# A hybrid attention and MLP block on one core: the first tile by row blocks, the mixing output's products spread in front of the weighing, and the MLP's start laid over the last attention tile

## The chip, the core and the metric

The program runs on one core of one Trainium2 chip. The metric is device time in microseconds (us) of one execution. The engines of the core are named as the profile names them: PE is TensorE's matmuls (PEld its weight loads), DVE VectorE, ACT ScalarE, POOL GpSimd, SP SyncE, which here only starts DMA transfers.

## The reference

One decoder layer for 2048 tokens of width 1024, in float32, cut to what matters here:

```
hn = rmsnorm(h, g_mix_pre)
z = hn @ w_in                                # 1024 x 1604
q, k, v, qi, ki, w, zp = split(z)            # rope on q, k, qi, ki
score = sum_h w[h] * relu(qi[h] @ ki.T)      # causal, 4 index heads
sel = top_k(score, 256)                      # keys kept for each query
attn = softmax(q @ k[sel].T) @ v[sel]        # 8 heads of 64, 2 kv heads
pool = pool_mixer(zp)
mix = concat(attn, pool) @ w_o               # 1024 x 1024
h = h + rmsnorm(mix, g_mix_post)
m = square(relu(rmsnorm(h, g_mlp_pre) @ w_up)) @ w_down      # hidden 4096
h = h + rmsnorm(m, g_mlp_post)
h = h + rmsnorm(sigmoid(h @ w_ple_gate) * (p @ w_ple_proj), g_ple_post)
```

Nearly every large product is written as three products of a high and a low float32 part (high by high, high by low, low by high).

## The kernel before, in words

The work stands in the program for each engine in its order, by hand, with semaphores between engines. A planner fills in the search for the kept keys (a threshold found in 32 rounds, each a count over the scores on DVE and on ACT) at numbered spots of the two stages below.

**Projection stage**, 16 tiles of 128 tokens. At the start SP starts five small loads, x for tiles 0 and 1, and the eight row blocks of w_in (128 rows each, w_in_raw). ACT makes each block's high part (w_in_hi, L986), DVE its low part (w_in_lo, L1442). DVE first computes the angles of the rotations (L1242 to L1256), for which ACT then takes the sine (L910). x is squared (L956), scaled (L1262) and transposed by PE (L1703) into hnT_hi (ACT, L941) and hnT_lo (DVE, L1267). Then PE computes four column groups of z one after the other, each over all eight row blocks (L1732).

**Attention stage**, 16 tiles of 8 heads, each head in 1 to 4 blocks of up to 512 keys; a step is one block of one head. In a step PE makes scores of a later step (L1754, L1755), transposes the probabilities of the step after next (L1840, turn_probs), and weighs the values with those of this step (L1854, weigh), for which it waits until ACT has copied them out of PSUM (probsT, L1071). DVE adds the mask to the scores as they come (L1484) and runs its half of the search round (L1346, then L1354 and L1363); ACT runs the exponential (L1058) and its half of the round (L968). After weigh come the index products of the search (L1754, L1755 with qi), and at the last block of heads 2 to 5 four products of the mixing output of the tile before (w_o, L1874, output_projection), 16 for a tile.

**MLP stage**, 4 chunks of 512 tokens. Weights come through a ring of two w_raw buffers of 1 MB, and are split into pieces (w_hi by ACT, L1114, w_lo by DVE, L1554) that PE takes one by one (L1732); the input hn_lo, hn_hi is loaded from DRAM and split (L1119, L1574). Before its first piece the program does the whole tail of tile 15: transpose of the attention output, its 16 output products, norms, the transposes of tiles 14 and 15 (L1891), their stores, and then the loads of the MLP (L740, L704).

Of the kernel before, what the change touches and what calls it, by code (L numbers as in the profile page):

```python
# [7 lines left out]
P = 128  # L8
F32 = mybir.dt.float32
# [8 lines left out]
Q_HEADS = 8  # L18
# [29 lines left out]
def hybrid_block(nc, x, p, positions, g_mix_pre, w_in, w_pool, pool_scale, w_o, g_mix_post,  # L48
# [32 lines left out]
    with ExitStack() as ctx:  # L81
# [80 lines left out]
        sbB("score_tail_kept", [P, S])  # L162
        block_max = sbB("block_max", [P, 2, 4])
# [12 lines left out]
        kept = sbB("kept", [P, S])  # L176
        drop = sbB("drop", [P, 2, S], BF16)
        weighed = sbB("weighed", [P, 3, 512])
# [14 lines left out]

        w_raw = sbC("w_raw", [P, 2, 2048])
        w_hi = sbC("w_hi", [P, 4, 1024], F32R)
        w_lo = sbC("w_lo", [P, 4, 1024], F32R)
        hn_hi = sbC("hn_hi", [P, K, CH], F32R)
        hn_lo = sbC("hn_lo", [P, K, CH], F32R)
        square = sbC("square", [P, 2, CH])
# [4 lines left out]
        hid_hi = sbC("hid_hi", [P, QF, CH], F32R)  # L204
        hid_lo = sbC("hid_lo", [P, QF, CH], F32R)
        g_mlp_row = sbC("g_mlp_row", [P, D])
        g_ple_row = sbC("g_ple_row", [P, D])
        p_in = sbC("p_in", [P, CT, PLE])
# [8 lines left out]
        w_in_ld = [sem("w_in_ld_low"), sem("w_in_ld_high")]  # L217
# [200 lines left out]

        AHEAD_BLOCKS = 2
# [74 lines left out]

        def mix_bank(i, n):
            return n if i == T - 1 else 0

        def norm_bank(i, n):
            return 2 + n if i >= T - 2 else 0
# [62 lines left out]
        def _(sp):  # L562
            def row_over_partitions(dst, src):
                return sp.dma_start(dst, src.to_broadcast([P, D]))

            sp.dma_start(pos_i[:], positions[0].rearrange("(t p) -> p t", p=P),
                         allow_slow_non_contiguous=True).then_inc(small_ld, 16)
            for dst, src in ((g_pre_col, g_mix_pre), (pool_scale_col, pool_scale), (g_mlp_col, g_mlp_pre)):
# [4 lines left out]
            def load_x(i, u):  # L573
                sp.dma_start(x_in[:, u, :], x_tiles[i]).then_inc(x_ld[u], 16)

# [3 lines left out]

            load_x(0, 0)  # L580
            load_x(1, 1)
            for k in range(K):
                sp.dma_start(w_in_raw[:, k, :], w_in[0, k * P:(k + 1) * P, :]).then_inc(w_in_ld[k // (K // 2)], 16)
# [65 lines left out]

            sp.wait_ge(zp_ps, T)  # L650
# [15 lines left out]
            for m, (H, b) in enumerate(steps):  # L666
# [16 lines left out]
                for t in mask_load_at.get(m, ()):  # L683
                    load_mask(t)
            load_pool(T - 1)
            store_h2(T - 2)
            load_x_row(T - 1)
            for i in range(T - 3, T):
                if i == T - 1:
                    store_h2(i)  # L690
                store_hn2T(i)

            sp.wait_ge(h2_st, 16 * T)
            hold()
            sp.wait_ge(hn2T_st, 16 * T)
            hold()
            loads = [0]

            def load_raw(width, src):
                n = loads[0]  # L700
                loads[0] += 1
                if n >= 2:
                    sp.wait_ge(w_lo_rdy, 2 * (n - 2) + 2)
                sp.dma_start(w_raw[:, n % 2, :].rearrange("p (k f) -> p k f", f=width), src).then_inc(raw_ld[n % 2], 16)  # L704

            def load_up(q, n):
                f = QF * q + 2 * n
                load_raw(2 * P, w_up[0, :, P * f:P * (f + 2)].rearrange("(k q) f -> q k f", q=P))

            def load_down(q, n):  # L710
                half, f = n // 2, QF * q + 4 * (n % 2)
                load_raw(512, w_down[0, P * f:P * (f + 4), 512 * half:512 * (half + 1)].rearrange("(a q) d -> q a d", q=P))

            def load_gate(n):
                half, k = n // 2, 4 * (n % 2)
                load_raw(512, w_ple_gate[0, P * k:P * (k + 4), 512 * half:512 * (half + 1)].rearrange("(a q) d -> q a d", q=P))

            def load_embed():
                n = loads[0]
                loads[0] += 1  # L720
                sp.wait_ge(w_lo_rdy, 2 * (n - 2) + 2)
                for k in range(KP):
                    sp.dma_start(w_raw[:, n % 2, :].rearrange("p (h k d) -> p h k d", h=2, k=KP)[:, :, k, :],
                                 w_ple_proj[0, P * k:P * (k + 1), :].rearrange("q (h d) -> q h d", h=2)).then_inc(embed_ld, 16)

            def load_tail():
                for n in range(GATE // 2):
                    load_gate(n)
                load_embed()

            for c in range(NCH):
                for q in range(QUARTERS):
                    if q == 2:
                        if c > 0:
                            sp.wait_ge(pT2_ps, 2 * c)
                            sp.wait_ge(out_st, 16 * CT * c)
                        sp.dma_start(p_in[:], p[0, 0, bass.ts(c, CH), :].rearrange("(a q) d -> q a d", q=P)).then_inc(p_ld, 16)
                        sp.dma_start(h2[:], h2_dram[bass.ts(c, CH), :].rearrange("(a q) d -> q a d", q=P)).then_inc(h2_ld, 16)
                    if c == 0 and q == 0:
                        sp.dma_start(hn_lo[:].bitcast(F32), hnT_dram[:, :, bass.ts(0, CH)]).then_inc(hn2T_ld, 16)  # L740
# [1326 lines left out]
```

## Time and profile before

| | |
|---|---|
| median of 3 runs | 3249.56 us (3245.02 to 3249.63) |
| the profiled execution's own time | 3245.62 us |
| its span | 3243.8 us |
| PE, DVE, ACT, POOL busy | 2958.4, 1719.7, 1384.8, 390.2 us |
| mean granted PE clock | 0.945 |

The span runs from the first to the last instruction; the execution's own time has 1.8 us more. Busy shares are means over stages that have different limits.

### The profile page before, as it was taken

The numbers are of one execution on the slowest core, as the hardware profiler recorded it, in microseconds if no ns is written. First come the engines' busy times: TensorE is split into PE (matmuls) and PEld (weight loads), VectorE is DVE, ScalarE is ACT, GpSimd is POOL, SyncE is SP. The second block draws the span as 40 slices with busy tenths as digits, with TensorE's granted clock in tenths as the row PEclk, the third lists the DMA queues.
The fourth block names the chain that finished last, engine by engine and source line by source line (L and its number), as shares of the span: only waits on it lengthen the run. The fifth ranks groups of instructions, "written<-read, shape, count | busy, mean of one in ns | idle before, by whom it ended". The sixth has DMA issues, their size and how long they took to land.

```text
span 3243.8 us, 37680 instructions
## 1 busy us (share of the span) xinstructions
PE 2958.4 (91%) x14264; PEld 2407.2 (74%) x14264; DVE 1719.7 (53%) x3405; ACT 1384.8 (43%) x2202; POOL 390.2 (12%) x447
## 2 busy tenths in 40 slices
PE   5999977788788898899699999999999999999987
PEld 4887755566666676787588888888888888888875
DVE  3376778686777776832333344533445334453344
ACT  3252546575747547655322243322433224332232
POOL 1233331213040040000000001000010000100001
PEclk9999988889897887899899999999999999999998
DMA  3111142111110110111424233333323333233321
GB/s 122 61 49 54 38 126 69 36 59 44 40 50 28 41 41 11 45 33 43 149 91 134 94 117 104 117 126 102 117 97 124 124 104 117 92 130 123 103 92 39
DMA packets 224627, 266.50 MB, mean 82 GB/s; under 512 B 58176, under 2 KB 160320, under 8 KB 224448
## 3 DMA queue, kind: packets, MB, share of 16 engines
q1 hardware_dynamic: 222144, 255.72, 25.0%
q10 hardware_dynamic: 2304, 8.39, 0.6%
q8 instruction: 113, 1.85, 0.2%
q14 instruction: 66, 0.54, 0.1%
HBM read 224.07 MB, written 40.01 MB: 81 GB/s over the span
## 4 chain that ended last, share of the span: by engine, by line
PE 79%; DVE 7%; issue 7%; ACT 4%; POOL 2%; DMA 1%; SPq 0%; DVEq 0%; ACTq 0%; POOLq 0%
PE bank L1732 58%; PE bank L1874 6%; PE bank L1854 6%; PE bank L1754 3%; PE bank L1840 2%; PE bank L1755 2%; ACT kept L968 2%; DVE kept L1346 1%; PE bank L1703 1%; DVE probs L1484 1%; ACT probsT L1071 1%; POOL score L868 1%; DVE too_few L1354 1%; DMA w_in_raw<-in_w_in 1%; ACT score_tail L968 0%
## 5 line engine op out<-in xcount | busy, mean ns | idle before, releaser
L1554 DVE TENSOR_TENSOR w_lo<-w_raw,w_hi 128x1024 fp32r<-128x1024 f32 x296 | 361.5, 1222 | 582.2 <-ACT w_hi L1114 582.1
L1114 ACT CAST w_hi<-w_raw 128x1024 fp32r<-128x1024 f32 x296 | 308.5, 1043 | 661.4 <-PE bank L1732 641.5
L1854 PE MATMUL bank<-values,probsT 128*128 128x64 f32 x2176 | 335.3, 301 | 150.9 <-ACT probsT L1071 124.2
L1854 PEld LDWEIGHTS bank<-values,probsT 128*128 128x128 f32 x2176 | 314.6, 220 | 177.3 <-ACT probsT L1071 163.6
L1732 PE MATMUL bank<-hn_hi,w_hi 128*128 128x512 f32 x1024 | 400.2, 391 | 20.8 <-DVE hn_lo L1574 20.8
L1732 PE MATMUL bank<-hn_hi,w_lo 128*128 128x512 f32 x1024 | 398.9, 390 | 0.0
L1732 PE MATMUL bank<-hn_lo,w_hi 128*128 128x512 f32 x1024 | 398.9, 390 | 0.0
L1732 PE MATMUL bank<-w_hi,hid_hi 128*128 128x512 f32 x1024 | 398.7, 389 | 0.0
L1732 PE MATMUL bank<-w_hi,hid_lo 128*128 128x512 f32 x1024 | 398.4, 389 | 0.0
L1732 PE MATMUL bank<-w_lo,hid_hi 128*128 128x512 f32 x1024 | 398.4, 389 | 0.0
L1484 DVE CUSTOM_DVE_ANT_0 probs<-bank,mask 128x384 f32<-128x384 f32 (+3 forms) x320 | 193.7, 607 | 234.3 <-PE bank L1755 232.5
L968 ACT ACTIVATE kept<-score,threshold 128x1024 bf16<-128x1024 f32 (+4 forms) x160 | 251.9, 1574 | 112.2 <-DVE threshold L1363 91.8
L1346 DVE TENSOR_SCALAR_CACHE_REDUCE kept<-score,threshold 128x896 bf16<-128x896 f32 (+4 forms) x160 | 267.6, 1673 | 0.7
L1172 ACT ACTIVATE square<-bank 128x512 f32<-128x512 f32 x128 | 76.5, 598 | 405.5 <-PE bank L1732 405.4
L1874 PE MATMUL bank<-wo_sb,mixT_t 128*128 128x512 f32 x512 | 247.0, 628 | 2.2 <-ACT h_t L1036 1.1
L1630 DVE CAST hid_hi<-square 128x512 fp32r<-128x512 f32 x128 | 56.1, 438 | 360.3 <-ACT square L1174 360.3
L1732 PEld LDWEIGHTS bank<-hn_hi,w_hi 128*128 128x128 f32 x1024 | 192.6, 188 | 61.0 <-DVE w_lo L1554 21.2
L1732 PEld LDWEIGHTS bank<-hn_hi,w_lo 128*128 128x128 f32 x1024 | 192.5, 188 | 40.0
L1732 PEld LDWEIGHTS bank<-hn_lo,w_hi 128*128 128x128 f32 x1024 | 192.7, 188 | 39.5
L1732 PEld LDWEIGHTS bank<-w_hi,hid_hi 128*128 128x128 f32 x1024 | 192.2, 188 | 40.1
L1732 PEld LDWEIGHTS bank<-w_hi,hid_lo 128*128 128x128 f32 x1024 | 192.2, 188 | 39.8
L1732 PEld LDWEIGHTS bank<-w_lo,hid_hi 128*128 128x128 f32 x1024 | 192.2, 188 | 39.7
(200 smaller groups left out, 4983.1 us busy)
## 6 DMA issues: line engine op xcount, KB each, us to landing
w_raw<-in_w_up SPq DMA_DIRECT2D x64, 1024.0 KB, 5.7
w_raw<-in_w_down SPq DMA_DIRECT2D x64, 1024.0 KB, 5.0
w_raw<-in_w_ple_gate SPq DMA_DIRECT2D x16, 1024.0 KB, 5.1
x_in<-in_x SPq DMA_DIRECT2D x16, 512.0 KB, 3.6
q_t<-q_scratch SPq DMA_DIRECT2D x32, 256.0 KB, 3.7
x_t<-in_x SPq DMA_DIRECT2D x16, 512.0 KB, 4.3
h_scratch<-h_t SPq DMA_DIRECT2D x16, 512.0 KB, 2.9
hnT_scratch<-hn2T_t SPq DMA_DIRECT2D x16, 512.0 KB, 3.8
```

Of the source, the lines that this page charges most:

```text
L968: nc.scalar.activation(junk[:, 0:P * (t + 2)], score_of(t + 1), ACT.Sign, scale=-1.0, bias=threshold[:, 1:2].bitcast(F32), accum_out=below ...
L1114: nc.scalar.copy(piece_parts(p, w_hi[:, p % 4, :]), raw_piece(p)).then_inc(w_hi_rdy, 1)
L1172: nc.scalar.activation(square[:, f % 2, :], bank[:, UP[q % 2][f % 2], :], ACT.Relu).then_inc(relu2_step, 1)
L1346: nc.vector.tensor_scalar(junk[:, 0:P * (t + 1)], score_of(t), threshold[:, 0:1].bitcast(F32), -float(P), ALU.is_lt, ALU.add, accum_out=be ...
L1484: nc.vector.tensor_tensor_reduce(out=probs[:, H % 3, o:o + w], in0=bank[:, ring_bank[("s", H, b)], 0:w], in1=mask[:, i % 2, o:o + w], scal ...
L1554: nc.vector.tensor_tensor(piece_parts(p, w_lo[:, p % 4, :]), raw_piece(p), piece_parts(p, w_hi[:, p % 4, :]).bitcast(F32), ALU.subtract).t ...
L1732: ins = nc.tensor.matmul(dst, lhs[a], rhs[b], start=(first and n == 0), stop=(last and n == 2))
L1754: nc.tensor.matmul(dst, hi, k_parts[:, key, o:o + w], start=True, stop=False)
L1755: return nc.tensor.matmul(dst, lo, k_parts[:, key, o:o + w], start=False, stop=True)
L1840: last = nc.tensor.transpose(bank[:, 1 + m % 3, a * P:(a + 1) * P], probs[:, H % 3, o + a * P:o + (a + 1) * P], ident[:])
L1854: last = nc.tensor.matmul(bank[:, 4, h * HEAD:(h + 1) * HEAD], probsT[:, m % 3, a * P:(a + 1) * P], values[:, kt, HEAD * kv:HEAD * (kv + 1 ...
L1874: last = nc.tensor.matmul(bank[:, mix_bank(i, n), :], mixT_t[:, k, :], wo_sb[:, k, n * 512:(n + 1) * 512], start=(k == 0), stop=(k == K - 1))
```

## The change

Three places of the program change; no arithmetic is added or left out.

Start: x of tile 0, g_pre_col and four row blocks are loaded first, with a semaphore for each row block; the angles and the sine are computed behind tile 0's products; PE takes tile 0's products row block by row block for all four column groups. Middle: the output products of a tile are laid out one to three to a step over the steps of heads 2 to 5 (tiles with one block a head: eight in one step) and they and the index products stand ahead of weigh. Seam: chunk 0's input and the first two weight buffers are loaded at the start of tile 15, split in its last eight steps, and the tail of tile 15 is called piece by piece between the MLP's first pieces. The buffers are laid out anew so that what is loaded early lies over what is no longer used.

```
+            def project_first_tile():
+                for k in range(K):
+                    if k % 4 == 0:
+                        pe.wait_ge(hnT_lo_rdy, k // 4 + 1)
+                    pe.wait_ge(w_in_lo_rdy, k + 1)
+                    for b, lo, hi, done_sem in (...four column groups...):
+                        last = split_product(...)
+                    if k == 5:
+                        transpose_x(1)
@@ order of DVE at the start (ACT alike)
             norm(0, 0)
+            split_weights(range(0, 1))
+            evacuate_hnT(0, 0)
+            evacuate_hnT(0, 1)
+            split_weights(range(1, 4))
+            norm(1, 1)
+            split_weights(range(4, K))
+            evacuate_hnT(1, 0)
+            evacuate_hnT(1, 1)
+            rotations()
+            norm(2, 0)
@@ a step of PE in the attention stage
+                for i_mix, n, k in mix_at.get(m, ()):
+                    output_projection(i_mix, n, range(k, k + 1))
+                search_part(EARLY_SPOTS + m)
                 weigh(m)
-                search_part(EARLY_SPOTS + m)
-                    if h in (2, 3):
-                        output_projection(i - 1, 0, range(4 * (h - 2), 4 * (h - 1)))
-                    if h in (4, 5):
-                        output_projection(i - 1, 1, range(4 * (h - 4), 4 * (h - 3)))
@@ SP, at the first step of tile 15
+                    load_hn(0)
+                    load_up(0, 0)
+                    load_up(0, 1)
@@ ACT, a step of tile 15
+                if m > FIRST_PARTS:
+                    act.wait_ge(ring_ps, ring[LAST_SCORE] + 1)
+                split_input(0, first_input(m))
+                for n in first_weights(m):
+                    split(n)
+            def attention_tail(p):          # PE's; called behind piece p
+                if p == 0:
+                    transpose_o(T - 1)
+                if p in (1, 2):
+                    output_projection(T - 1, p - 1, range(K))
+                if p == 3:
+                    for n in range(2):
+                        transpose_hn2(T - 2, n)
+                if p == 9:
+                    for n in range(2):
+                        transpose_hn2(T - 1, n)
```

The order of DVE's instructions from the end of the angles on (COPY rot) before, in the first microseconds of the program:

```order
L1256 COPY rot<-turns 128x1
L1260 TENSOR_SCALAR ms<-ss 128x1
L1262 TENSOR_SCALAR x_in<-x_in,rstd 128x1024
L1442 SCALAR_TENSOR_TENSOR w_in_lo<-w_in_raw,g_pre_col,w_in_hi 128x1604 x8
L1260 TENSOR_SCALAR ms<-ss 128x1
L1262 TENSOR_SCALAR x_in<-x_in,rstd 128x1024
L1267 TENSOR_TENSOR hnT_lo<-bank,hnT_hi 128x512 x2
```

And DVE from its first instruction on in the changed kernel:

```order
L1298 TENSOR_SCALAR ms<-ss 128x1
L1300 TENSOR_SCALAR x_in<-x_in,rstd 128x1024
L1506 SCALAR_TENSOR_TENSOR w_in_lo<-w_in_raw,g_pre_col,w_in_hi 128x1604
L1305 TENSOR_TENSOR hnT_lo<-bank,hnT_hi 128x512 x2
L1506 SCALAR_TENSOR_TENSOR w_in_lo<-w_in_raw,g_pre_col,w_in_hi 128x1604 x3
L1298 TENSOR_SCALAR ms<-ss 128x1
L1300 TENSOR_SCALAR x_in<-x_in,rstd 128x1024
L1506 SCALAR_TENSOR_TENSOR w_in_lo<-w_in_raw,g_pre_col,w_in_hi 128x1604 x4
L1305 TENSOR_TENSOR hnT_lo<-bank,hnT_hi 128x512 x2
L1487 CAST pos_f<-pos_i 128x16
```

Tile 0's hnT_lo moved from behind eight low parts to behind one, and the angles from the front to behind tile 1's hnT_lo.

PE before, two steps of tile 5 (heads 2 and 3, two blocks of 384 keys a head), from scores to scores:

```order
L1754 MATMUL bank<-k_parts,q_hi 128x384
L1755 MATMUL bank<-k_parts,q_lo 128x384
L1840 MATMUL bank<-ident,probs 128x128 x3
L1854 MATMUL bank<-values,probsT 128x64 x3
L1874 MATMUL bank<-wo_sb,mixT_t 128x512 x4
L1754 MATMUL bank<-k_parts,q_hi 128x384
L1755 MATMUL bank<-k_parts,q_lo 128x384
L1840 MATMUL bank<-ident,probs 128x128 x3
L1818 MATMUL bank<-ident,q_t 128x128 x4
L1854 MATMUL bank<-values,probsT 128x64 x3
```

PE in the changed kernel, the same two steps:

```order
L1833 MATMUL bank<-k_parts,q_hi 128x384
L1834 MATMUL bank<-k_parts,q_lo 128x384
L1934 MATMUL bank<-ident,probs 128x128 x3
L1968 MATMUL bank<-wo_sb,mixT_t 128x512 x3
L1948 MATMUL bank<-values,probsT 128x64 x3
L1833 MATMUL bank<-k_parts,q_hi 128x384
L1834 MATMUL bank<-k_parts,q_lo 128x384
L1934 MATMUL bank<-ident,probs 128x128 x3
L1912 MATMUL bank<-ident,q_t 128x128 x4
L1968 MATMUL bank<-wo_sb,mixT_t 128x512 x3
L1948 MATMUL bank<-values,probsT 128x64 x3
```

Of the eight products of one half (n = 0), which stood as four behind the weighing of every second step, three, three and two now stand ahead of the weighing in three steps that follow each other.

ACT before, from the last copy of a mixing output in tile 15 to the tail:

```order
L1036 COPY h_t<-bank 128x512
L1071 COPY probsT<-bank 128x512 x4
L1052 COPY hn2T_t<-bank 128x512
L1071 COPY probsT<-bank 128x512 x3
L1052 COPY hn2T_t<-bank 128x512
```

ACT in the changed kernel, from the same copy on:

```order
L1086 COPY h_t<-bank 128x512
L1137 COPY probsT<-bank 128x512
L1124 ACTIVATE hn_hi<-hn_lo,g_mlp_col 128x512 x2
L1137 COPY probsT<-bank 128x512
L1124 ACTIVATE hn_hi<-hn_lo,g_mlp_col 128x512 x2
L1137 COPY probsT<-bank 128x512
L1124 ACTIVATE hn_hi<-hn_lo,g_mlp_col 128x512 x2
L1137 COPY probsT<-bank 128x512
L1102 COPY hn2T_t<-bank 128x512
L1124 ACTIVATE hn_hi<-hn_lo,g_mlp_col 128x512 x2
L1137 COPY probsT<-bank 128x512
L1119 CAST w_hi<-w_raw 128x1024
```

Eight splits of the MLP's input and the first of weights now stand between the copies for which PE's last steps wait.

## Rows read from the trace of the kernel before

**Rows 1.** Busy time by stage; PE, PEld, DVE, ACT, POOL, then clock, DMA share, GB/s.

```profile
0.00:60.40 60.40, 24.83 (x113) 20.69 (x114) 23.64 (x36) 20.63 (x25) 4.24 (x51) 1.00 0.43 149
60.40:330.00 269.60, 254.82 (x1358) 215.36 (x1357) 147.17 (x407) 94.86 (x228) 88.25 (x128) 0.98 0.18 55
330.00:1350.00 1020.00, 847.46 (x4251) 658.97 (x4250) 763.50 (x1900) 615.73 (x1056) 204.71 (x206) 0.86 0.16 47
1350.00:1530.80 180.80, 180.64 (x1226) 150.17 (x1225) 78.84 (x193) 97.40 (x155) 13.54 (x10) 1.00 0.14 43
1530.80:1585.70 54.90, 24.82 (x81) 14.78 (x81) 11.46 (x18) 19.05 (x30) 3.99 (x4) 0.72 0.37 115
1585.70:3243.80 1658.10, 1625.84 (x7243) 1347.28 (x7241) 695.04 (x854) 537.14 (x709) 75.43 (x48) 0.99 0.34 109
```

**Rows 2.** PE's waits over the whole span: us in total, times, longest.

```profile
PE bank L1854 <- ACT probsT L1071: 124.2, 77, 5.7
...
PE bank L1732 <- DVE hn_lo L1574: 20.8, 1, 20.8
```

**Rows 3.** Timeline of the start: start, duration, engine, line, operation, [idle before <- releaser].

```profile
6.83 0.17 DVE L1242 CAST pos_f<-pos_i 128x16 f32<-128x16 int32 x1 [6.83 <-DMA w_pool_sb<-in_w_pool]
...
26.38 6.20 ACT L986 ACTIVATE w_in_hi<-w_in_raw,g_pre_col 128x1604 fp32r<-128x1604 f32 x4 [1.66 <-DMA w_in_raw<-in_w_in]
28.04 7.29 DVE L1442 SCALAR_TENSOR_TENSOR w_in_lo<-w_in_raw,g_pre_col,w_in_hi 128x1604 fp32r<-128x1604 f32 x4 [0.57 <-ACT w_in_hi L986]
...
37.52 0.77 PE L1732 MATMUL bank<-w_in_hi,hnT_hi 128*128 128x512 f32 x1 [20.16 <-DVE hnT_lo L1267]
...
42.74 0.39 PE L1732 MATMUL bank<-w_in_hi,hnT_hi 128*128 128x512 f32 x1
```

**Rows 4.** DMA of the first 30 us: GB/s in 40 slices.

```profile
GB/s 0 0 1 7 8 3 17 269 195 344 322 344 437 424 411 419 445 411 411 445 419 411 436 396 411 419 419 411 411 428 419 428 411 399 389 126 0 0 0 0
```

**Rows 5.** Chain that ended last, first 200 us: start, duration, what.

```profile
54.83 11.07 PE bank L1732 x48
...
75.73 11.10 PE bank L1732 x48
```

**Rows 6.** Timeline in tile 5: two rounds of the search, then a step with output products.

```profile
660.33 1.41 DVE L1346 TENSOR_SCALAR_CACHE_REDUCE kept<-score,threshold 128x1152 bf16<-128x1152 f32 x1
...
663.01 1.41 DVE L1346 TENSOR_SCALAR_CACHE_REDUCE kept<-score,threshold 128x1152 bf16<-128x1152 f32 x1
...
673.40 3.65 PE L1874 MATMUL bank<-wo_sb,mixT_t 128*128 128x512 f32 x8
...
677.55 0.56 DVE L1484 CUSTOM_DVE_ANT_0 probs<-bank,mask 128x384 f32<-128x384 f32 x1 [2.03 <-PE bank L1755]
```

**Rows 7.** DVE's waits for scores, 330 to 1350 us: total, times, longest.

```profile
DVE probs L1484 <- PE bank L1755: 150.4, 79, 6.9
```

**Rows 8.** Timeline: first and last of 34 stops of DVE behind output products.

```profile
491.36 0.56 DVE L1484 CUSTOM_DVE_ANT_0 probs<-bank,mask 128x384 f32<-128x384 f32 x1 [3.71 <-PE bank L1755]
...
1293.51 0.56 DVE L1484 CUSTOM_DVE_ANT_0 probs<-bank,mask 128x384 f32<-128x384 f32 x1 [1.89 <-PE bank L1755]
```

**Rows 9.** Timeline of the seam.

```profile
1528.20 2.79 PE L1854 MATMUL bank<-values,probsT 128*128 128x64 f32 x24
1528.40 0.59 ACT L1071 COPY probsT<-bank 128x512 f32<-128x512 f32 x1 [0.16 <-PE bank L1840]
...
1533.63 14.00 PE L1874 MATMUL bank<-wo_sb,mixT_t 128*128 128x512 f32 x32 [0.81 <-ACT mixT_t L1026]
...
1556.20 1.97 PE L1891 MATMUL bank<-ident,hn_t 128*128 128x128 f32 x8 [7.70 <-ACT hn_t L1047]
...
1575.87 1.04 ACT L1114 CAST w_hi<-w_raw 128x1024 fp32r<-128x1024 f32 x1 [17.07 <-DMA w_raw<-in_w_up]
1576.82 5.00 ACT L1119 ACTIVATE hn_hi<-hn_lo,g_mlp_col 128x512 fp32r<-128x512 f32 x8
...
1578.98 0.77 PE L1732 MATMUL bank<-hn_hi,w_hi 128*128 128x512 f32 x1 [20.81 <-DVE hn_lo L1574]
```

More of the change, by code:

```diff
@@ L214, in hybrid_block @@
         mlp_stack.close()
-        w_in_ld = [sem("w_in_ld_low"), sem("w_in_ld_high")]
+        g_pre_ld = sem("g_pre_ld")
+        w_in_ld = [sem(f"w_in_ld_{k}") for k in range(K)]
         w_in_hi_rdy = sem("w_in_hi_rdy")
@@ L417, in hybrid_block @@
                 q_turn_at.setdefault(head_first[Q_HEADS * i + 2 + n], []).append((i + 1, n))
+        mix_at = {}
+        for i in range(1, T):
+            for n in range(2):
+                first = Q_HEADS * i + 2 + 2 * n
+                places = range(head_first[first] + 1, head_first[first + 2])
+                for k in range(K):
+                    mix_at.setdefault(places[k * len(places) // K], []).append((i - 1, n, k))
         AHEAD_BLOCKS = 2
@@ L687, in _ @@
             load_x_row(T - 1)
[L688 to L729, printed above, removed]
+            store_hn2T(T - 3)
             for c in range(NCH):
@@ L1059, in exp, with split, split_input @@
                                      accum_out=denom[:, i % 2, h:h + 1]).then_inc(exp_rdy, 1)
+            def split(p):
+                n = p // 2
+                if n in embed_loads:
+                    act.wait_ge(embed_ld, 32 * embed_loads[n] + 32)
+                else:
+                    act.wait_ge(raw_ld[n % 2], 16 * raw_count(n))
+                if p >= 4:
+                    act.wait_ge(piece_done, p - 3)
+                nc.scalar.copy(piece_parts(p, w_hi[:, p % 4, :]), raw_piece(p)).then_inc(w_hi_rdy, 1)
+            def split_input(c, parts):
+                for n in parts:
+                    act.wait_ge(hn2T_ld, 16 * c + 16)
+                    nc.scalar.activation(hn_hi[:, n, :], hn_lo[:, n, :].bitcast(F32), ACT.Identity,
+                                         scale=g_mlp_col[:, n:n + 1]).then_inc(hn_hi_rdy, 1)
             split_queries(0, 0)
@@ L1215, in last_tail @@
                     store_out(c, a)
-            split(0)
-            split_input(0, range(HN))
-            for n in range(1, AHEAD):
-                split(n)
             for c in range(NCH):
@@ L1281, in rope @@
             def rope(i, u):
+                dve.wait_ge(trig_rdy, 1)
                 dve.wait_ge(za_ev, i + 1)
@@ new lines, in _ @@
+            split_weights(range(0, 1))
+            evacuate_hnT(0, 0)
+            evacuate_hnT(0, 1)
+            split_weights(range(1, 4))
+            norm(1, 1)
+            split_weights(range(4, K))
+            evacuate_hnT(1, 0)
+            evacuate_hnT(1, 1)
+            rotations()
+            norm(2, 0)
+            for i in range(1, T):
+                if i >= 2:
+                    evacuate_hnT(i, 1)
+                rope(i - 1, (i - 1) % 2)
+                early_part(4 * i - 1)
@@ L1678, in last_tail @@
                     output(c, a)
-            split(0)
-            split_input(0, range(HN))
-            for n in range(1, AHEAD):
-                split(n)
             for c in range(NCH):
```

356 lines of the change are left out of this document (216 added, 140 removed).

## The prediction

> **What bounds the kernel now.** I read three views. First the stages [rows 1]: PE is busy in nearly all of the projection stage, of tiles 14 and 15, and of the MLP, but not at the start (24.8 of 60.4 us), in the middle (847 of 1020) and at the seam between attention and MLP (24.8 of 54.9). The clock says the same: 1.00 and 0.98 where PE is dense, 0.86 in the middle, 0.72 at the seam. So these three places hold what there is to win, about 36, 173 and 30 us of idle PE, and the change touches just these. Second PE's waits [rows 2]: the largest is weigh for ACT's copy of the probabilities, 124.2 us in 77 stops; the seam's longest stop is one of 20.8 us. Third the timelines of the places.
>
> **Start.** Before: DVE does the angles first (6.8 to 12.1 us), ACT and DVE then split all eight row blocks, at 1.6 and 1.9 us each with the later four starting at 26.4, when the transfer has landed, and PE has its first product at 37.5, behind the eighth low part and tile 0's hnT_lo [rows 3]. Tile 0's products end 5.5 us behind the start of the chain's piece at 54.83, at 60.4 [rows 5]. After, worked out with the same durations: x lands near 4.4 (its transfer is issued 3.6 us earlier), square, scale and transposes end near 9.3. The row blocks come 2.0 us apart (0.82 MB at 411 GB/s [rows 4]), from about 6 on. ACT: block 0 to 8.6, hnT_hi to 10.5. DVE: block 0's low part to 10.5, hnT_lo to 11.9, first half 11.2. So PE starts at about 11.3. From there the low parts are ready at 14.0, 15.9, 17.8, 21.2, 23.1, 25.0, 26.9 (tile 1's scaling between them costs 1.5). PE needs 2.4 us a row block at full clock and 4.2 at half. The row at 37.52 shows products at half clock (0.77, then 0.43 apart) until 42.74, after a long idle stretch [rows 3]; I take the same 5 us of half clock here. Row blocks then end at 15.4, 18.2, 20.6, 23, 25.4, 27.8, then 0.9 of transposes, 31.1, 33.5. PE sets the pace, DVE is 6 us ahead. Tile 0 ends at 33.5 instead of 60.4: 26.9 us.
>
> Part is given back: the angles (5.3 us on DVE) now stand behind tile 1's hnT_lo (34.9), so the sine comes at 40.3 to 40.8, and ACT's copy of the pool rows stands behind it on ACT and ends at 41.4. PE, done with tile 1's first column group at 39.0, waits 2.4 us for it (transpose_pool). Behind the sine also stand square_x of tile 2 and the evacuation of tile 1's first group; both are wanted later than 50 us, so they are covered. A load of ACT's function table (the sine moves behind other functions) goes into the 4.6 us in which ACT waits for the angles; uncovered it would cost 1.3.
>
> By the Trainium skill (page "ScalarE: Activation LUTs", section "What ACT_TABLE_LOAD costs") a switch costs the load of 1.28 us and a drain of 1.38, 2.66 together. By that page the cover still holds, and the start would give the same; uncovered it would be 1.4 us less. No row here shows the drain.
>
> Behind this, the projection stage is dense (255 of 270 us [rows 1]) and tile by tile equal (the chain's pieces at 54.83 and 75.73 are 20.9 apart [rows 5]), so the shift lasts. **Start: 26.9 - 2.4 = 24.5, taken as -24**; bounds -18 (loads land 2 us later, half clock for longer, table load uncovered) and -27.
>
> **Seam.** Before, from the end of the weighing at 1530.8 to the end of piece 0 at 1585.7 are 54.9 us. PE's work in it at full clock: transposes 0.4 + 0.5, output products 14.0, sixteen transposes of norms 2.0, piece 0 24 x 0.228 = 5.5: 22.4. So 32.5 us are idle or slow: 20.8 + 7.7 + 1.6 idle [rows 9], 2.4 half clock. After, the loads (1562 to 1576 before) lie some 60 us earlier on an SP queue and DMA that idle there; input and weights are split before the last weighing; piece 0 follows the last transposes. In the tail each link has a piece of 5.5 us of PE as its cover: mixT_t is wanted 11.5 us behind the end of the weighing and ready near 10.6; the norm's chain before (1547.5 to 1556.2, 8.7 us) now has pieces 3 to 8. SP's later stores of tiles 13 to 15 stand in front of weight loads; the first holds load 2 to about 2 us behind the weighing, landed by 9, wanted by 22. Covered.
>
> What is new: in the last seven steps ACT has seven copies (4.1), eight input splits (5.0), one hn2T copy (0.6), two weight splits (2.1): 11.8 us, while PE has about 1.3 us of work a step, 9.2 (0.93 for four weighings, the rest transposes [rows 9]). Weigh waits for each copy. With the mixing copies just ahead (1.4) PE loses 2.6 to 6; I take 4.5. **Seam: 32.5 - 4.5 = -28**; bounds -22 and -32.
>
> **Middle.** In a search step DVE sets the pace: its rounds are 2.68 us apart (660.33 and 663.01). A group of four output products takes 3.5 us of PE in one step, and DVE then stands for the next scores, here 2.03 [rows 6]. Of about 49 such groups between 330 and 1350 us 34 are followed by a stop of DVE, of 0.3 to 6.2 us, 82.6 in all, the first at 491.36, the last at 1293.51 [rows 8]; that is over half of DVE's 150.4 us behind scores [rows 7]. A product is 0.87 us. Spread, a stop of 2.0 for four becomes 1.2 for three, 0.3 for two, none for one. Half a tile loses 4.0 before; with two blocks a head (3, 3, 2) 2.6 after, with three (2, 2, 1, 2, 1) 0.9, with four 0.3. Over tiles 4 to 7, 8 to 11, 12 and 13 that is 11 + 25 + 15 = 51 us, if all 40 pairs of groups were such stops, 81 us of them. I count 52: from 82.6 I leave out 8 in tiles 1 to 3 (there eight products now form one group: nothing gained) and 23 where index products keep PE busy anyway. 51 x 52/81 = 33. What the order ahead of weigh adds is unknown: the work that it puts in front covers ACT's copy in those steps (at most 124.2, in steps without such work nothing), but it also puts the weighing, and so the next scores, no earlier than before: in a step that DVE or ACT sets it gives nothing. **Middle: -32**, bounds 0 (ACT's rounds, which wait for DVE's thresholds, take over) and -83 (every stop behind the groups goes).
>
> The output products in tiles 14 and 15 gain nothing: PE is busy 180.6 of 180.8 us there [rows 1].
>
> **Sum.** Against the profiled execution's own time, 3245.6 (3.9 below the median of the runs shown, within their spread): 3245.6 - 24 - 28 - 32 = 3161.6, forecast 3162.
>
> **Rivals.**
> A: the middle gives nothing. For it: PE's stops are for ACT, and ACT has to wait for DVE's thresholds; taking PE's clumps away may just move the wait. Against: the stops behind the groups are seen. 3245.6 - 24 - 28 = 3194.
> B: the clock follows. The middle has 0.86, with both of TensorE's levels in it; denser steps keep PE at 2.4 GHz, where four weighings and scores take half as long, and the stops for ACT shrink too. If half of the 124 us goes beside the 33, less overlap, the middle gives 83: 3110. This is also what the page "TensorE: Matmul & The Clock Gate" of the Trainium skill (section "A second HAM failure mode: psum-queue depth-cycling") leads to: short stops between groups of products cost clock, and by it fewer of them give more than their own length. The rows at 37.52 and 42.74 show both levels, behind an idle stretch and behind work; they do not show how much the middle would hold.
> C, slower: products in front of weigh lengthen steps in which PE is at half clock and already full. About 160 products of tiles 4 to 13 move into other steps; a product costs 0.87 us at full clock and 1.73 at half, and all of them at half clock without any cover would be 277 us against the 139 at full. It takes over once the spread costs more than 52/160 = 0.33 us a product net; at 0.45 the time is 3266. Against: such steps are few, since DVE waits for PE in only 79 of some 240 blocks, and PE's clock comes back when it is busy.
> D: the start is given back later (search rounds tied to DVE, not to PE's tiles) or the last steps wait longer: 3182.
>
> **Chances.** Forecast with D's shades (3130 to 3190) 0.68, A 0.14, B 0.14, C 0.04. The forecast's own range is 3130 to 3190; with A's and B's near parts, 3118 to 3198 leaves out no more than 0.2. The median of three runs can tell 0.2%, 6.5 us, from no change. Only C ends above that line: faster 0.96, same 0.01, slower 0.03.
>
> **What would show it.** First product near 11 us and tile 0's products done near 34, a stop of about 2 us before the pool rows' transposes. In the middle DVE's waits for scores down from 150 to about 110, output products one to three in a row, and the stage some 30 us shorter; a clock well above 0.86 speaks for B, unchanged DVE waits for A, longer rounds for C. At the seam no stop over 3 us, PE waits for probsT of some 4 us in tile 15's last steps, and hn_lo loaded while tile 15 runs. Wrong would be: a stop of PE at pieces 1 to 12 behind mixT_t or hn2T, or row blocks that land much later than 2 us apart.

## The result, and the profile after

The changed kernel takes 3136.31 us (median of 4 runs, 3132.34 to 3139.56) against 3248.64 for the kernel before (4 runs, 3245.02 to 3249.63): ratio 0.9656, interval 0.9639 to 0.9672, about 112 us less. The profiled execution took 3133.52, with a span of 3131.6 against 3243.8. The forecast was 3162, with a range of 3118 to 3198. Of the experiments further down, one execution of e9 took 11380 us and one of e12 16280 us; their medians contain these, their ratios do not (without it e9's median is 3124.45).

The stages of the changed kernel, with the columns of [rows 1]: start, rest of the projection, middle, tiles 14 and 15, seam, MLP.

```profile
0.00:33.70 33.70, 24.10 (x111) 20.18 (x112) 18.28 (x15) 18.55 (x17) 3.68 (x50) 1.00 0.77 266
33.70:306.90 273.20, 254.79 (x1358) 215.28 (x1358) 152.72 (x427) 98.16 (x236) 89.04 (x129) 0.98 0.17 54
306.90:1258.80 951.90, 806.05 (x4246) 632.44 (x4246) 765.60 (x1902) 614.71 (x1057) 204.96 (x206) 0.89 0.17 51
1258.80:1442.50 183.70, 182.56 (x1233) 152.22 (x1232) 88.57 (x203) 106.16 (x167) 13.97 (x10) 0.99 0.21 62
1442.50:1450.20 7.70, 7.70 (x29) 6.33 (x29) 3.38 (x5) 1.66 (x4) 0.00 (x0) 0.75 0.78 224
1450.20:3131.60 1681.40, 1649.13 (x7293) 1355.21 (x7291) 695.20 (x856) 545.42 (x724) 79.44 (x52) 0.99 0.33 108
```

The first stage is cut at 33.70, 0.45 us before tile 0's last product ends. Its clock of 1.00 is no reading: the trace has no record of the clock before 16.2 us, and the distance of the products there (0.43 us until 16.2, then 0.23) shows 1.2 GHz first. The middle holds the same work in both (4246 products of PE against 4251) and is 68.1 us shorter: 41.4 of it is less PE busy time, at a clock of 0.89 in place of 0.86, and 26.7 less idle time. The seam is 7.7 us of dense work, and its output products now lie in the MLP's row.

PE's waits over the whole span, to be read beside [rows 2]:

```profile
PE bank L1948 <- ACT probsT L1137: 97.0, 66, 5.6
...
PE bank L1813 <- DVE hnT_lo L1305: 14.0, 9, 2.4
```

The stop of 20.8 us for hn_lo is gone, and the wait for probsT is down from 124.2 to 97.0.

The timeline of the start, to be read beside [rows 3]:

```profile
7.24 1.63 ACT L1019 ACTIVATE w_in_hi<-w_in_raw,g_pre_col 128x1604 fp32r<-128x1604 f32 x1 [1.60 <-DMA w_in_raw<-in_w_in]
7.48 1.94 PE L1782 MATMUL bank<-ident,x_in 128*128 128x128 f32 x8 [7.48 <-DVE x_in L1300]
...
11.54 0.80 PE L1813 MATMUL bank<-w_in_hi,hnT_hi 128*128 128x512 f32 x1 [2.12 <-DVE hnT_lo L1305]
12.10 5.49 DVE L1506 SCALAR_TENSOR_TENSOR w_in_lo<-w_in_raw,g_pre_col,w_in_hi 128x1604 fp32r<-128x1604 f32 x3
...
33.76 0.39 PE L1813 MATMUL bank<-w_in_hi,hnT_lo 128*128 128x512 f32 x1
...
40.82 1.28 ACT L1043 ACT_TABLE_LOAD   x1 [5.02 <-DVE rot L1501]
43.06 0.69 PE L1782 MATMUL bank<-ident,zp_rows 128*128 128x128 f32 x4 [3.34 <-ACT zp_rows L1025]
```

The first product starts at 11.54 us, where 11.3 was worked out, and the last of tile 0 (the row at 33.76) ends at 34.15 (33.5). The table load stands behind ACT's 5.02 us of waiting, not in them. In the kernel before, the load for the same sine did run ahead of its wait:

```profile
0.72 1.28 ACT L910 ACT_TABLE_LOAD   x1 [0.72 <-PEq L2056]
...
12.12 0.42 ACT L910 ACTIVATE trig<-turns 128x256 f32<-128x256 f32 x1 [10.12 <-DVE rot L1256]
```

The last steps of tile 15 and the first piece of the MLP, to be read beside [rows 9]:

```profile
1437.83 1.10 PE L1948 MATMUL bank<-values,probsT 128*128 128x64 f32 x8 [0.66 <-ACT probsT L1137]
1438.62 0.59 ACT L1137 COPY probsT<-bank 128x512 f32<-128x512 f32 x1
1439.26 3.40 PE L1948 MATMUL bank<-values,probsT 128*128 128x64 f32 x16 [0.33 <-ACT probsT L1137]
...
1440.46 3.48 DVE L1592 TENSOR_TENSOR w_lo<-w_raw,w_hi 128x1024 fp32r<-128x1024 f32 x3
...
1442.46 1.06 PE L1987 MATMUL bank<-ident,hn_t 128*128 128x128 f32 x4
1443.17 0.78 PE L1813 MATMUL bank<-hn_hi,w_hi 128*128 128x512 f32 x1
...
1444.09 0.69 DVE L1570 TENSOR_TENSOR o_sb<-bank,inv_denom 128x512 f32<-128x512 f32 x1
```

PE stops for 1.2 us in all (one more stop of 0.16 ahead of these rows). The rows show something else: the last 16 weighings take 3.40 us where 24 took 2.79 before, and the first product takes 0.78 us, so PE is at 1.2 GHz here, until 1446.3. From 1442.5 to 1560 PE waits for nothing.

**The ledger.** How far the changed kernel is ahead: PE's last product of tile 0's projection ends 26.2 us earlier (60.37 before, 34.15 after), that of tile 1's 21.1 us earlier (81.30 and 60.19). From there one event, followed tile by tile in both traces (DVE's o_sb, one for each tile), gives 23.1 at attention tile 0, 91.2 at tile 13, 87.2 behind tile 15. The first transposes of p_in in the MLP start at 1917.8 before and 1799.9 after, 117.9 ahead, of which 1.9 had been lost again in chunk 0. So: start 21 to 23, middle 68, last steps -4, tail at the seam +32.6. Then something is lost that the prediction did not have: the three further chunks take 408.9 us each in place of 407.0, 7.4 us over four chunks. The spans agree: 23.1 + 68.1 - 4.0 + 32.6 - 7.4 = 112.4 against 112.2.

### The profile page after: what moved, and what is told of

It is laid out like the page before. It is cut to its first block, busy times and chain, and to the rows that moved or that the text cites. A ratio compares the mean times of both kernels' runs of the same rounds, so it can differ in the third digit from the quotient of the medians.

```text
span 3131.6 us, 37711 instructions
## 1 busy us (share of the span) xinstructions
PE 2924.3 (93%) x14264; PEld 2381.7 (76%) x14264; DVE 1723.7 (55%) x3405; ACT 1384.7 (44%) x2203; POOL 391.1 (12%) x447
## 4 chain that ended last, share of the span: by engine, by line
PE 77%; issue 8%; DVE 7%; ACT 4%; POOL 2%; DVEq 0%; ACTq 0%; POOLq 0%
PE bank L1813 59%; PE bank L1968 5%; PE bank L1948 5%; PE bank L1833 2%; PE bank L1934 2%; PE bank L1834 2%; ACT kept L1005 1%; DVE kept L1385 1%; POOL score L908 1%; PE bank L1782 1%; DVE probs L1557 1%; ACT score_tail L1005 1%; DVE too_few L1393 1%; ACT probsT L1137 1%; DVE kept L1437 0%
## 5 line engine op out<-in xcount | busy, mean ns | idle before, releaser
L1948 PE MATMUL bank<-values,probsT 128*128 128x64 f32 x2176 | 322.0, 293 | 123.5 <-ACT probsT L1137 97.0
L1813 PEld LDWEIGHTS bank<-hn_hi,w_lo 128*128 128x128 f32 x1024 | 191.9, 187 | 45.1
```

Of the source, the lines that this page charges most:

```text
L1813: ins = nc.tensor.matmul(dst, lhs[a], rhs[b], start=(first and n == 0), stop=(last and n == 2))
L1948: last = nc.tensor.matmul(bank[:, 4, h * HEAD:(h + 1) * HEAD], probsT[:, m % 3, a * P:(a + 1) * P], values[:, kt, HEAD * kv:HEAD * (kv + 1 ...
```

## The experiments

Twelve kernels. The first four part the middle's two edits; medians stand against 3247.11 us for the kernel before in the same job.

**e1, the change with its middle put back** (a step of PE as before):

```
+                weigh(m)
                 search_part(EARLY_SPOTS + m)
-                weigh(m)
...
+                    if h in (2, 3):
+                        output_projection(i - 1, 0, range(4 * (h - 2), 4 * (h - 1)))
...
```

> The changed kernel with the middle put back: groups of four output products and the index products behind the weighing. Theory 1 (three independent parts, middle worth 68 us by the drift of the attention outputs' times between the two traces): 3136 + 68 = 3204. Theory 2 (part of the 68 us is a gift of the earlier start, for example another phase of the search against the tiles): less than 40 us slower than the changed kernel, under 3176.

Measured: 3207.72 us, ratio 0.9876 (0.9861 to 0.9891). The middle is worth 71 us in the changed kernel. (The traced execution of e1, 3199.03, is 9 us below its median.)

**e2, the kernel before with the middle alone** (output products spread, they and the index products ahead of weigh):

```
+                for i_mix, n, k in mix_at.get(m, ()):
+                    output_projection(i_mix, n, range(k, k + 1))
+                search_part(EARLY_SPOTS + m)
                 weigh(m)
-                search_part(EARLY_SPOTS + m)
...
-                    if h in (2, 3):
-                        output_projection(i - 1, 0, range(4 * (h - 2), 4 * (h - 1)))
...
```

> The kernel before with the middle's edit alone. Theory 1: 3248 - 68 = 3180. Theory 2: less than half of it, over 3214.

Measured: 3181.10 us, ratio 0.9794 (0.9777 to 0.9810), 66 us. The middle gives the same with and without the other two places, to within 5 us.

**e3, spreading, but behind the weighing**: `mix_at` and its loop stand directly behind weigh. That is not spreading alone: the output products now stand ahead of the index products, where before they stood behind them.

> The kernel before with the output products spread one to three a step, but they and the index products still behind the weighing. If the spread is the cause, as the prediction had it, 3248 - 33 = 3215, DVE's waits for scores down by some 40 us and the order worth the rest; if the clock follows the spread, nearer 3190; if the order is the cause, within 10 us of 3248.

Measured: 3240.56 us, ratio 0.9978 (0.9969 to 0.9988). 6.6 us, where the forecast had 33.

**e4, order alone**: groups of four and index products, both ahead of weigh.

> The kernel before with groups of four output products and the index products ahead of the weighing, not spread. If ACT's late copies are what the order covers, 35 us faster (3213) with PE's waits for probsT well under 124 us; by the prediction's reckoning 0 to 5 us faster.

Measured: 3205.98 us, ratio 0.9873 (0.9859 to 0.9888), 41 us. The order, which the forecast reckoned at nothing, carries most; 66 - 41 - 7 = 18 us appear only with both together.

**e5 and e6 part the order**: index products alone ahead (e5), output products in fours alone ahead (e6).

```
@@ e5
+                search_part(EARLY_SPOTS + m)
                 weigh(m)
-                search_part(EARLY_SPOTS + m)
@@ e6
+                if last_of(H, b) and i >= 1:
+                    if h in (2, 3):
+                        output_projection(i - 1, 0, range(4 * (h - 2), 4 * (h - 1)))
...
                 weigh(m)
```

> The kernel before with the index products of the search put ahead of the weighing, the mixing output's products left in fours behind it. Both moves together, in fours, gave 41 us. Theory 'the index products carry it' (they stand in nearly every step of tiles 1 to 14, so they cover ACT's copy in many more of the 76 stops than 34 groups of output products do): -30 to -41, 3206 to 3217. Theory 'the output products carry it': 0 to -10, 3237 to 3247, with PE's waits for probsT near 120.

> The kernel before with the mixing output's products, still in fours, put ahead of the weighing, the index products left behind it. Theory 'the index products carry it': 0 to -10, 3237 to 3247. Theory 'the output products carry it': -30 to -41, 3206 to 3217, and ACT's waits for the mixing output (h_t) down from 74 to about 40. If e5 and this one add up to 41 the two moves act on different stops; if the sum is well over 41 they cover the same ones.

Measured against 3246.92: e5 3239.33 us, ratio 0.9982 (0.9972 to 0.9993); e6 3215.59, ratio 0.9905 (0.9890 to 0.9920). The output products carry 31 us, the index products some 8 (by the interval 2 to 9). The two add up to nearly the 41 of e4. (e5's ten executions run from 3236 to 3248; the traced one, 3245.68, is no faster than that of the kernel before.) The timeline of the kernel before in tile 5, around the group of [rows 6]:

```profile
672.68 0.88 PE L1854 MATMUL bank<-values,probsT 128*128 128x64 f32 x6 [0.73 <-ACT probsT L1071]
...
676.49 0.73 PE L1754 MATMUL bank<-k_parts,q_hi 128*128 128x384 f32 x1
...
680.57 0.88 PE L1854 MATMUL bank<-values,probsT 128*128 128x64 f32 x6 [1.05 <-ACT probsT L1071]
...
681.28 3.22 PE L1874 MATMUL bank<-wo_sb,mixT_t 128*128 128x512 f32 x7
```

And the same place in e6:

```profile
674.83 3.60 PE L1874 MATMUL bank<-wo_sb,mixT_t 128*128 128x512 f32 x8
...
675.52 0.47 ACT L1071 COPY probsT<-bank 128x384 f32<-128x384 f32 x1
...
678.27 0.78 PE L1854 MATMUL bank<-values,probsT 128*128 128x64 f32 x6
...
678.86 0.42 PE L1754 MATMUL bank<-k_parts,q_hi 128*128 128x384 f32 x1
...
679.60 0.56 DVE L1484 CUSTOM_DVE_ANT_0 probs<-bank,mask 128x384 f32<-128x384 f32 x1 [0.63 <-PE bank L1755]
...
680.97 3.60 PE L1874 MATMUL bank<-wo_sb,mixT_t 128*128 128x512 f32 x8
```

Before, PE first stands for the copy (1.05 us at 680.57), and then makes four products: the next scores have both in front of them. In e6 the copy (675.52) lies under the products, and weighing and scores follow without a stop. From group to group it is 7.88 us before (673.40 to 681.28) and 6.14 in e6; DVE stands 0.63 us in place of 2.03.

**e7 and e8 look for the MLP's loss** in hn_hi's new place: first in its region in the kernel before (e7), moved by 8 KB in the changed kernel (e8).

> The kernel before with hn_hi put first in the MLP's region of SBUF (it stood behind the three weight buffers), nothing else. Theory 'the place of hn_hi costs the changed kernel its 7.4 us in the MLP': its products take 391 to 393 ns in place of 389 and each chunk 408.9 us in place of 407.0, so +6 to +8, 3253 to 3255. Theory 'something else in the changed kernel does it' (other neighbours, other transfers during the chunk): 0, each chunk 407.0.

> The changed kernel with the two gain rows put ahead of hn_hi, so that hn_hi starts 8 KB later in each partition. Theory 'hn_hi's place costs 7.4 us': -5 to -8, 3128 to 3131, hn_hi's products at 389 ns, 407.0 us a chunk. Theory 'something else does it': 0, 408.9 us a chunk.

Measured: e7 3248.75 us, ratio 1.0007 (0.9998 to 1.0017); e8 3132.50, within the runs of the changed kernel, its first and last p_in transposes at 1799.8 and 3027.2 as there (1799.9 and 3027.3). The place alone costs nothing. The theory falls. (In e7 all these buffers still start multiples of 1 KB apart; the expectation for e9 says otherwise, wrongly. In e8 their distances modulo 1 KB are those of the changed kernel. So neither run says anything on the layout theory of e9.)

**e9, the changed kernel with ACT's copy ahead of the sine and the gaps in the layout filled**:

```
+            copy_pool_rows(0)
+            square_x(2)
...
             nc.scalar.activation(trig[:], turns[:], ACT.Sin)
-            copy_pool_rows(0)
-            square_x(2)
...
-        sbC("rest_of_values", [P, P + T * IDX_HEADS + 32])
+        sbC("rest_of_values", [P, P + T * IDX_HEADS + 64])
-        sbC("rest_of_weighed", [P, 640])
+        sbC("rest_of_weighed", [P, 768])
```

> The changed kernel with two edits, in places that don't touch, so that the trace parts them. First, ACT copies the pool rows of tile 0 and squares x of tile 2 ahead of the sine instead of behind it: PE's stop of 3.34 us for them at 43.06 us should be gone, and tile 1's part of the stage should end 3 to 4 us earlier; if the table load only moves the stop to the rotations, nothing is won. Second, the two gaps in the MLP's layout are filled up, so that hn_lo, w_lo, w_hi and w_raw start at the same offset modulo 1 KB as hn_hi (as all of them do in the kernel before, and in none of the two runs in which only hn_hi moved). Theory 'the offsets of the two operands against each other cost 1.9 us a chunk': chunks of 407.0 us, hn_hi's products at 389 ns, -7 us. Theory 'it is not the layout': 408.9 and 393. Both right: 3122 to 3127; only the first: 3129 to 3132; none: 3133 to 3137.

Measured: 3125.07 us, ratio 0.9625 (0.9612 to 0.9638) against 3246.59, the fastest of all. Both edits worked. The start of e9, and then its hn products in the MLP from 2400 to 2600 us (columns: count, busy us, mean ns, idle before):

```profile
39.78 0.60 PE L1782 MATMUL bank<-ident,zp_rows 128*128 128x128 f32 x4
...
41.04 1.28 ACT L1045 ACT_TABLE_LOAD   x1 [3.52 <-DVE rot L1501]
```

```profile
L1813 PE MATMUL bank<-hn_hi,w_lo 128*128 128x512 f32 x132 | 51.4, 389 | 0.0
L1813 PE MATMUL bank<-hn_hi,w_hi 128*128 128x512 f32 x131 | 51.0, 389 | 0.0
```

The same groups in the changed kernel, 2282 to 2582 us:

```profile
L1813 PE MATMUL bank<-hn_hi,w_hi 128*128 128x512 f32 x188 | 73.9, 393 | 0.0
L1813 PE MATMUL bank<-hn_hi,w_lo 128*128 128x512 f32 x188 | 73.5, 391 | 0.0
L1813 PE MATMUL bank<-hn_lo,w_hi 128*128 128x512 f32 x188 | 73.0, 388 | 0.0
```

PE's stop for the pool rows is gone, and the first chunk's p_in transposes stand at 1794.6, 5.3 us earlier than in the changed kernel; 1.9 of that is chunk 0, so 3.4 is left of the start. (At the end of tile 1's projection it is 4.9 us, 55.34 against 60.19.) First to last they are 1221.8 us apart, against 1227.4.

PE's clock just behind the place of the stop, in the changed kernel and in e9:

```profile
43.50:46.90 3.40, 3.40 (x10) 2.73 (x9) 2.11 (x8) 2.67 (x6) 0.55 (x1) 0.51 0.00 0
```

```profile
43.50:46.90 3.40, 3.40 (x23) 2.93 (x21) 2.47 (x6) 2.20 (x8) 2.36 (x3) 1.00 0.29 116
```

Without the stop the clock stays at 2.4 GHz there.

**e10 and e11 test a rival to cover: ACT's stop.** ACT copies each half of the mixing output one block later; PE's order stays. e10 is the kernel before so changed, e11 is e9 so changed.

```
-                    if h == 4 and i >= 1:
+                    if h == 4 and 1 <= i < 4:
                         evacuate_mix(i - 1, 0)
...
+                if b == 1 and i >= 4 and h in (4, 6):
+                    evacuate_mix(i - 1, h // 2 - 2)
```

> The kernel before with one thing moved on ACT: from tile 4 on it squares and copies the two halves of the mixing output one block later (block 1 of heads 4 and 6 instead of block 0), so that it doesn't stand still for a group of four output products that PE has just begun. PE's order is untouched. Theory 'ACT's stop is what the order costs' (behind the weighing, the four products end last, ACT stands for them, 73.9 us in 18 stops between 330 and 1350, and the next copy of probabilities and count of the search come late by as much; ahead of it, 37.6): -20 to -35, 3212 to 3227, ACT's waits for the output products under 20 us. Theory 'cover' (the products ahead of the weighing win because PE works while ACT copies the probabilities, whatever ACT does with the mixing output): within 8 us of nothing, 3239 to 3251, PE's waits for probsT unchanged near 124.

> The kernel of e9 with e10's move on ACT. ACT still waits 32.5 us in 12 stops for the mixing output's products in the changed kernel. Theory 'ACT's stop': -10 to -25 against e9. Theory 'cover': within 5 us of e9.

Measured: e10 3263.46 us, ratio 1.0053 (1.0039 to 1.0067); e11 3151.38, ratio 0.9705 (0.9692 to 0.9718), 26 us slower than e9. Neither theory had that: 'cover' allowed 8 us in e10 and 5 in e11. ACT's waits in tiles 8 to 13, first in the kernel before (541.5 us long), then in e10 (544.8 us):

```profile
ACT kept L968 <- DVE threshold L1363: 53.2, 43, 6.2
ACT h_t L1033 <- PE bank L1874: 43.1, 11, 6.9
```

```profile
ACT kept L968 <- DVE threshold L1365: 67.0, 35, 5.8
...
ACT h_t L1033 <- PE bank L1876: 23.3, 7, 5.1
```

ACT's stop for the output products did halve, and nothing was won by it: ACT waits for DVE's thresholds instead. So in these tiles its stop was not the cost. Of the 17 us that e10 loses 13.5 are in tiles 4 to 7 (67.9 us a tile against 64.5), where blocks are few and the later copy comes closer to the next half, which goes into the same bank. There ACT's waits for the output products fall from 26.4 to 8.0 us and those for the thresholds rise from 19.7 to 45.1; which wait makes the loss was not parted. So for tiles 4 to 7 the two runs leave the rival open; what speaks against it there is PE's gap, counted further down.

**e12, e9 with the index products behind weigh again.**

> The kernel of e9 with the index products of the search put back behind the weighing; the mixing output's products stay spread and ahead of it. Theory 'the index products add their own small part' (6 us in e5): +4 to +8 against e9, 3129 to 3133. Theory 'they matter more once the output products are spread' (spread, order and index together gave 66, while output products ahead in fours gave 31, spreading 7, index 6: 22 are left over): +10 to +20, 3135 to 3145. Theory 'what is left over belongs to spread and order together, and the index products are covered anyway': within 3 us of e9, with PE's gap ahead of weighings in tiles 8 to 11 unchanged.

Measured: 3136.89 us, ratio 0.9654 (0.9641 to 0.9666) against 3248.48; 12 us slower than e9, near the low end of the second theory. Once the output products are spread, the index products ahead are worth 12 us, against some 8 alone, and of the 66 of e2 some 16 are left (66 - 31 - 7 - 12) for spreading and order together. The 12 us are no cover of a copy: PE's gap ahead of the weighings of heads 2 to 5 in tiles 8 to 11 is 3.2 us in e12 and 3.1 in e9. What grows is DVE's wait for the index products' own scores (its rows weighed and score, shown further down for e9), 34.5 us in e9 and 57.5 in e12.

## Why the prediction was right, and where not

**Start: right, 3 us short.** The first product came out within 0.3 us and the end of tile 0's products within 0.7, so 26.2 us were gained there where 26.9 were foreseen. The sum had -24.5 behind the pool rows' stop, and -21.1 was measured behind tile 1: 5.1 us were given back in place of 2.4. What failed is "A load of ACT's function table ... goes into the 4.6 us in which ACT waits for the angles; uncovered it would cost 1.3". In the changed kernel the load stands behind that wait, so the stop for the pool rows was 3.34 us where 2.4 were foreseen.

It is no rule that a load waits with its activation: in the kernel before it ran 10 us ahead of the sine. There one wait stands in front of the sine in the program, in the changed kernel three, and its trace has a separate wait instruction (L1042) that ends at 40.79, just before the load. That the number of waits decides, and not that the early load is the first of the program, is argued; no run has the sine late with one wait.

The rest of what was given back, 1.8 us, is a second stretch of half clock behind the stop, which the sum did not have: granted clock 0.51 from 43.5 to 46.9, and 1.00 there in e9, where the stop is gone. e9 takes both away by two moved lines, 4.9 us at tile 1, of which 3.2 are left at attention tile 0. (The changed kernel itself goes from 21.1 there to 23.1; where it gains these 2 us was not parted.)

**Seam: right.** Tail +32.6 (foreseen 32.5), last steps -4.0 (4.5): 28.6 against 28. The second number is right for a partly different reason. The forecast had ACT's copies as its only cause; PE's stops there sum to 1.2 us, and half clock in the last 16 weighings costs some 1.5 more (3.40 us; 24 took 2.79 at full clock). The last 1.1 us is not PE's at all: at the end of its last weighing the lead is 88.3 (1530.99 and 1442.66), but o_sb, by which the ledger counts, waits on DVE behind three low parts of weights (the row at 1440.46) and is 87.2 ahead. The half clock in piece 0 is part of the tail's number.

**Middle: the sign right, size and cause wrong.** -68 in the trace against -32. Two steps failed. First "Spread, a stop of 2.0 for four becomes 1.2 for three, 0.3 for two, none for one", 33 us: e3 did that behind the weighing and gave 6.6. Second "in a step that DVE or ACT sets it gives nothing" for the order ahead of weigh: e4 gave 41. The first goes back to a reading: [rows 7] is only one of three rows in which DVE stands for scores. The index products' scores have rows of their own. For the kernel before, over the stretch used below:

```profile
DVE probs L1484 <- PE bank L1755: 148.6, 77, 6.9
DVE weighed L1333 <- PE bank L1755: 18.2, 22, 2.0
...
DVE score L1333 <- PE bank L1755: 6.9, 6, 3.2
```

The stretch runs from the first weighing of the stage to the first of head 3 of tile 13. In e3, in e9 and then (the first row alone) in e6 these waits of DVE are:

```profile
DVE probs L1492 <- PE bank L1763: 99.4, 63, 8.1
DVE weighed L1341 <- PE bank L1763: 37.8, 21, 7.6
...
DVE score L1341 <- PE bank L1763: 16.5, 9, 3.2
```

```profile
DVE probs L1557 <- PE bank L1834: 57.0, 77, 3.3
DVE weighed L1372 <- PE bank L1834: 25.8, 15, 7.0
...
DVE score L1372 <- PE bank L1834: 8.7, 6, 1.9
```

```profile
DVE probs L1484 <- PE bank L1755: 81.7, 65, 4.9
```

Spreading behind the weighing lowered the row of [rows 7] by 49 us, but raised the other two by 29, as the output products there stand ahead of the index products. Whether spreading would have given more with the index products first was not tried. The second step failed at "the next scores, no earlier than before". In e6 PE does not stand for the copy, so all that follows comes earlier: 6.14 us from group to group in place of 7.88, and the row of [rows 7] falls from 148.6 to 81.7 with the groups still of four.

The three rows summed, beside the length of that stretch and PE's share in it, for all kernels that differ in the middle:

| kernel | stretch, us | DVE waits for scores, sum of three | PE busy | PE idle | clock |
|---|---|---|---|---|---|
| e10 copy late | 929.9 | 190.3 | 762.6 | 167.3 | 0.83 |
| before | 912.9 | 173.7 | 750.7 | 162.2 | 0.85 |
| e5 index ahead | 911.2 | 172.0 | 751.9 | 159.3 | 0.84 |
| e1 middle put back | 909.4 | 170.2 | 744.1 | 165.3 | 0.85 |
| e3 spread | 906.7 | 153.7 | 742.2 | 164.5 | 0.86 |
| e6 output ahead in fours | 879.0 | 135.8 | 725.8 | 153.2 | 0.87 |
| e11 e9, copy late | 871.1 | 121.4 | 722.9 | 148.2 | 0.86 |
| e4 both of e5 and e6 | 869.7 | 127.1 | 724.5 | 145.2 | 0.86 |
| e12 spread, output ahead | 858.8 | 106.4 | 722.7 | 136.1 | 0.87 |
| e2 all of the middle | 845.3 | 94.9 | 713.7 | 131.6 | 0.87 |
| changed kernel | 842.8 | 91.0 | 707.3 | 135.5 | 0.88 |
| e9 same middle | 841.9 | 91.5 | 716.2 | 125.7 | 0.87 |

The windows behind it, first the kernel before and then the changed one:

```profile
439.10:1352.00 912.90, 750.69 (x3730) 577.51 (x3730) 686.64 (x1685) 566.74 (x946) 164.81 (x151) 0.85 0.16 46
```

```profile
419.00:1261.80 842.80, 707.29 (x3727) 549.53 (x3726) 687.48 (x1683) 564.93 (x942) 164.51 (x151) 0.88 0.17 49
```

DVE's busy time is the same in all (685 to 688), and the stretch shortens with its waits for scores, with hardly an exception down the table: 83 us less waiting, 70 less time. It is not one for one (e5 to e3: 18 less waiting, 4.5 less time; e3 to e6: 18 less waiting, 28 less time), so the sum orders the kernels but does not price an edit.

Why the two edits need each other is seen in PE's gap just ahead of a step's first weighing, summed over rows of the timeline. In tiles 4 to 7 the 16 steps with a group lose 16.9 us there before, 0.4 in e4. In tiles 8 to 11 the steps with a group lose only 2.9; the gap is in the 32 other steps of heads 2 to 5: 14.6 before, 14.1 in e4, 12.2 in e3, and 2.1 in e2. A product covers a copy only if it stands ahead of the weighing and in that step. That much is shown. It is not all: in tiles 8 to 11 e6 is 13.7 us faster in total (85.7 us a tile against 89.1), with these gaps only 3 us smaller. And that the remaining 16 to 18 us of interplay are all of this kind is argued.

**The clock.** Rival B's mechanism is part of the result. Of 70 us in that stretch 43 are less busy time for the same products and 27 less idle time. The trace's records of the granted clock have 283 us of the stretch at 1.2 GHz before and 198 in the changed kernel; PE works in 240 and 162 of them, and half of these 79 us is 39 of the 43. So for every microsecond of idle time gone PE gave back 1.6 more by running at 2.4 GHz for longer. That figure is one execution's: e9, with the same middle and the same length, splits its 71 us into 34.5 busy and 36.5 idle, 0.9 more for each. The Trainium skill, page "TensorE: Matmul & The Clock Gate", section "A second HAM failure mode: psum-queue depth-cycling", describes a kernel in which short stops of PE between groups of products made its clock swing, so that throughput fell while the median product kept its time at full clock. The granted clock of this stretch, 0.85 to 0.88 as the stops fell, agrees with the first part; no run here changes the clock by itself. The forecast counted B as a case by itself, where it was a factor on the main one, and so its sum lay low.

**MLP: not foreseen**, 7.4 us. The layout was taken as free. e9 shows that it is not, and e7 and e8 that it isn't hn_hi's place.

**The total.** That 3136 lies in the range is partly luck. The middle gave 36 us more than the sum had, and 7.4 of these went again in the MLP, where the sum had nothing. And inside the middle a term of 33 that measured 7 was more than made good by one put at nothing that measured 41.

**A, C and D** did not come. No spread product lengthened a tile (C): tiles 4 to 7, 8 to 11 and 12 to 13 take 60.0, 79.6 and 86.2 us each in the changed kernel (by o_sb), and 64.5, 89.1 and 92.5 before.

## What to carry to other kernels

An engine that stands for another's copy should have its independent work ahead of that wait, in small pieces and in every step that has such a wait; behind the wait the same work adds to the delay of all that follows. When an engine sets the pace, sum all rows in which it waits for the same producer before pricing an edit, for a wait that falls in one row may rise in another. And where the clock is below full, idle time that is removed is worth more than its length: here 1.9 to 2.6 times.

## What the runs showed of the hardware

- A load of ACT's function table can run ahead of the wait of the activation that needs it, or stand behind it. Before, it took 1.28 us at 0.72, and the sine came at 12.12 behind 10.12 us of idle ACT. In the changed kernel it took 1.28 us at 40.82, behind 5.02 us of idle ACT, and again at 41.04 in e9 behind 3.52. What decides was not parted: the late ones stand behind three waits, the early one had one and was the program's first load.
- Behind PE's stop of 3.34 us stand 3.4 us of half clock (granted clock 0.51 from 43.5 to 46.9 us); in e9, without the stop, it is 1.00 there.
- Where the operands lie matters to a product's time. In the changed kernel the MLP's buffers hn_lo, w_raw and w_lo start 896 bytes and w_hi 384 bytes beyond a whole multiple of 1 KB from hn_hi; the products with hn_hi as moving operand then take 393 and 391 ns, and 389 where all start at the same offset modulo 1 KB (the kernel before, and e9). Products of the same weights with hid stay at 389 in both. A different offset alone is not enough: hn_lo and w_hi lie 512 bytes apart modulo 1 KB in the changed kernel, and their products take 388. Which pair of buffers does it, and at what granularity, was not parted; e9 filled both gaps at once.
